# Two-layer hybrid decoder step: the first layer's projection opens with both slabs of its first pair, tile by tile

## The reference

```
mod = silu(c) @ ada_w[i] + ada_b[i]
h = rmsnorm(x, norm_pre_mix) * (1 + sc1) + sh1
proj = h @ w_in                       # gb, gc, hv, z (1024 each), xbc (1536), dt_raw (16)
xbc_c = silu(causal_conv4(xbc)); dt = softplus(dt_raw + dt_bias)
mix = concat(gb * causal_conv3(gc * hv), ssd(xbc_c, dt, ...)) @ w_out
x = x + g1 * rmsnorm(mix)
h = rmsnorm(x) * (1 + sc2) + sh2
f = swiglu(h) in layer 0, top-2-of-8 expert swiglu in layer 1
x = x + g2 * rmsnorm(f)
```

## Time and profile before

| What | Value |
|---|---|
| median of 3 executions | 2057.71 us (2055.87 to 2061.11) |
| profiled execution, its own time | 2059.96 us |
| span of the profiled execution | 2057.9 us |
| TensorE (matmul) busy | 1927.6 us, 94% |
| VectorE busy | 1233.8 us, 60% |
| ScalarE busy | 846.2 us, 41% |
| mean granted TensorE clock | 0.964 of full speed |

### The profile page before, as it was taken

One profiled execution on the slowest core, in us unless ns is written; L12 is line 12 of the kernel. 1 busy time (PEld: TensorE's weight loads), 2 busy tenths in 40 slices (PEclk: granted clock), 3 DMA queues, 4 the chain that ended last, 5 costly groups with the idle time before them and its releaser, 6 DMA issues.

```text
span 2057.9 us, 36163 instructions
## 1 busy us (share of the span) xinstructions
PE 1927.6 (94%) x13204; PEld 1716.4 (83%) x13204; DVE 1233.8 (60%) x1783; ACT 846.2 (41%) x1030; POOL 218.7 (11%) x317
## 2 busy tenths in 40 slices
PE   4999999999999999987999999996599999999994
PEld 3888998997999999986889989995487878888884
DVE  3677667645523232336776666656565566888886
ACT  4332222454422122234322222635355456777774
POOL 3101211200000000001102212100100000000020
PEclk8999999999999999997999999997699999999997
DMA  9642443354234333325624333423547567999994
GB/s 337 236 165 93 133 133 108 128 210 150 96 132 142 104 134 132 118 76 201 241 92 140 127 101 129 151 82 125 186 144 264 194 204 249 362 385 383 382 385 171
DMA packets 146670, 376.99 MB, mean 183 GB/s; under 512 B 9712, under 2 KB 47024, under 8 KB 146080
## 3 DMA queue, kind: packets, MB, share of 16 engines
q1 hardware_dynamic: 119824, 274.61, 38.8%
q0 software_dynamic: 26768, 101.28, 13.6%
HBM read 340.06 MB, written 35.80 MB: 183 GB/s over the span
## 4 chain that ended last, share of the span: by engine, by line
PE 85%; DVE 4%; issue 4%; DMA 3%; ACT 2%; POOL 1%; DVEq 0%; POOLq 0%; ACTq 0%; SPq 0%
PE ps L1913 35%; PE ps L1921 17%; PE ps L2235 17%; PE ps L2256 4%; PE ps L1956 2%; PE ps L2105 1%; DMA adaw<-w_ada 1%; PE ps L1966 1%; PE ps L1935 1%; PE ps L2108 1%; PE ps L2106 1%; PE ps L2093 1%; DMA rawr<-w_gu 1%; PE ps L1988 1%; POOL wreg L737 0%
## 5 line engine op out<-in xcount | busy, mean ns | idle before, releaser
L1913 PE MATMUL ps<-h_hi,whi 128*128 128x272 f32 x2304 | 485.2, 292 | 7.1 <-DVE h_lo L1236 7.1
L1913 PE MATMUL ps<-h_lo,whi 128*128 128x272 f32 x2304 | 479.1, 289 | 0.0
L1913 PEld LDWEIGHTS ps<-h_hi,whi 128*128 128x128 f32 x2304 | 363.5, 189 | 49.8 <-issue 29.5
L1746 DVE TENSOR_TENSOR wlr<-rawr,whr 128x2048 fp32r<-128x2048 f32 (+1 forms) x162 | 322.1, 1993 | 121.3 <-ACT whr L1041 117.7
L1184 DVE TENSOR_TENSOR wlo<-raw,whi 128x1024 fp32r<-128x1024 f32 (+1 forms) x180 | 229.3, 1274 | 255.2 <-ACT whi L781 252.7
L1913 PEld LDWEIGHTS ps<-h_lo,whi 128*128 128x128 f32 x2304 | 363.5, 189 | 0.0
L781 ACT CAST whi<-raw 128x1024 fp32r<-128x1024 f32 (+1 forms) x180 | 193.7, 1076 | 347.5 <-PE ps L1921 342.1
L1041 ACT CAST whr<-rawr 128x2048 fp32r<-128x2048 f32 (+1 forms) x162 | 269.1, 1667 | 155.6 <-PE ps L2256 87.6
L1921 PE MATMUL ps<-h_hi,wlo 128*128 128x272 f32 x2304 | 311.7, 288 | 0.0
L1921 PEld LDWEIGHTS ps<-h_hi,wlo 128*128 128x128 f32 x2304 | 297.9, 188 | 0.0
L2235 PE MATMUL ps<-whr,hu_hi 128*128 128x512 f32 (+1 forms) x432 | 168.3, 390 | 7.0 <-DVE yu L1810 4.5
(11 more groups left out here) (411 smaller groups left out, 2683.2 us busy)
## 6 DMA issues: line engine op xcount, KB each, us to landing
rawr<-w_gu SPq DMA_DIRECT2D x90, 1024.0 KB, 9.7
adaw<-w_ada POOLq DMA_DIRECT2D x48, 1024.0 KB, 8.9
rawr<-w_dn SPq DMA_DIRECT2D x54, 768.0 KB, 9.5
raw<-w_mix SPq DMA_DIRECT2D x64, 512.0 KB, 3.4
raw<-w_gu SPq DMA_DIRECT2D x44, 512.0 KB, 3.3
raw<-w_out SPq DMA_DIRECT2D x32, 512.0 KB, 3.3
y_rows<-tables POOLq DMA_DIRECT2D x26, 512.0 KB, 2.9
raw<-w_xbc SPq DMA_DIRECT2D x24, 512.0 KB, 3.8
```

Source lines behind the costliest of these rows:

```text
L1746: v.tensor_tensor(ring_group(wlr, g).rearrange("p k s c -> p s k c"), raw_group(g), ring_group(whr, g).bitcast(F32).rearrange("p k s c -> ...
L1913: mm(ps[:, 2 * s + half, 0:HALF], whi[:, s, k * P:(k + 1) * P], a[:, k, half * HALF:(half + 1) * HALF], start=(n < 2), stop=False)
```

## The change

```diff
@@ SyncE @@
                 if L == 0:
                     load_slab(0, 0, w_xbc[L, 0], SLAB)
-
-                    sp.wait_ge(ada_landed[KT - 2], 16)
                     load_slab(0, 1, w_xbc[L, 1], SLAB)
@@ ScalarE @@
                 make_rstd(NORMS * L + PRE_MIX, D, rstd)
                 if L == 0:
                     hi(0, 0, SLAB)
+                    hi(0, 1, SLAB)
                 modulate(L, 0, 0)
-                if L == 0:
-                    hi(0, 1, SLAB)
@@ VectorE @@
             lo(0, 0, SLAB)
+            lo(0, 1, SLAB)
...
                 dve.wait_ge(h_ready, (2 * L + 1) * KT)
-                if L == 0:
-                    lo(0, 1, SLAB)
                 narrow_take(L, 0)
@@ TensorE @@
-                        if L and i == 0:
+                        if i == 0:
                             if s == 0:
                                 first_pair(first["xbc"], h_ready, 2 * L * KT, lambda k: project(L, 0, k))
                                 by_token(L, 0, ps[:, 5, :]).then_inc(dt_done, 1)
-                        elif (i, s) == (0, 0):
-                            slab(first["xbc"], 0, KT, h_hi, h_lo, (h_ready, 2 * L * KT), lambda k: project(L, 0, k))
-                            by_token(L, 0, ps[:, 5, :]).then_inc(dt_done, 1)
                         else:
                             slab(i + first["xbc"], s, KT, h_hi, h_lo)
```

## The result

The changed kernel takes 2063.97 us (median of 20 executions, 2058.57 to 2070.49) against 2056.94 us of the kernel before (20 executions, 2052.0 to 2063.95): 7.0 us more by the medians. The ratio is 1.003, 95% interval 1.002 to 1.004, which is 4 to 8 us.

What follows compares the result with a forecast made beforehand. TensorE's chain was taken to bound the kernel, with the opening up to 35 us bound by full DMA engines. 1.36 + 0.4 + 2.3 + 3.0 = 7.06, taken as +7.1 on 2057.71, gave 2064.8 us, range 2060.0 to 2068.0.

Steps and rivals of the forecast that it cites:

- Part 1, bytes ahead of the last piece: Opening: slab (0, 1)'s 512 KB move ahead of the last `adaw` piece at 386 GB/s, delaying `mod` and first matmul, +1.36 us.
- Rival 3: Opening: GpSimd's queue sets the pace, so slab (0, 1) loads free and the piece still lands at 35.08; 2063.0 us, 5%.
- the sign that was named: Opening: the last piece of `adaw` lands at 36.4 to 37.2 us instead of 35.08.
- Part 1, the earlier slab (1, 0): Opening: slab (1, 0), issued earlier, shares the DMA engines with the last `adaw` piece, +0.4 us, upper end 2.7.
- Rival 2: Opening: SyncE's slabs take turns with the last piece from their issue on; landing beyond 38 us, 2067.1 us, 10%.
- Part 2, the splits: Ahead of `modulate`: ScalarE's second cast and VectorE's second subtraction fit in their idle time, 0 us.
- Part 3, the wait: Layer 0, TensorE's opening: only 2.84 us of work left over the 5.14 us dt chain, so +2.3 us waiting for `dA_ready`.
- Part 4, the clock: Layer 0 behind that wait: clock falls to 0.50, slowing the products of `dA` and slab (1, 0), +3.0 us.
- Rival 1: Behind layer 0's wait for `dA_ready`: the wait is too short for the clock to fall; 2061.8 us, 20%.
- What comes after: Behind slab (1, 0) and in later stages: the backlog makes no gap and the shift passes through, 0 us.
- the chances: Whole kernel, against a mark of 0.3% (6.2 us): slower 0.54, the same 0.44, faster 0.02.

## Why the prediction was right

The forecast was +7.1 us, 2064.8; measured were +7.0 and 2063.97. That the two agree to 0.1 us is luck: the interval is some 2 us wide on either side, the ratio alone gives 6.2 us, and a term that was too large stands beside a delay that was left out. The mechanism, bytes, wait and clock, held. Step by step:

- **Part 1, bytes ahead of the last piece: 1.36.** Right. The landing moved by 1.45 on the mean of four profiles against four, and by 2.74 for twice the bytes. Rival 3 (free beside GpSimd's queue) falls with that. With slab (1, 0) held back the step is 36.12 - 34.90 = 1.22. But the sign that was named, a landing at 36.4 to 37.2 us, was missed: it came at 36.09, and in the three runs that also load early at 36.31, 36.34 and 36.64. The sign had the 0.4 of the next item in it, and it started from 35.08, the latest of the four landings without the early load.
- **Part 1, the earlier slab (1, 0): 0.4, bounds 0 to 2.7.** Too large. Holding it back moved the landing by 0.2 us on the mean, within the scatter. Its bytes came about as late as supposed: issued from 31.58 us on, none before 35 us, 0.14 MB before 36 us. Rival 2 (turns from the issue on, beyond 38 us) falls. By the rule of the Trainium skill (DMA: Bandwidth & Descriptors, Queues, rings and completion order) the queues take turns; here the trace agrees for 16 to 20 us (52.2% and 50.2%) and 36 to 42 us (56.2% and 45.2%), and not for the first 3 to 4 us behind the issue.
- **Not in the sum: the clock before the first tile.** With the piece later, the eight matmuls on it mostly ran wholly at half clock (1.98 us), and the first matmul on `h` moved by 1.8 us on the mean where the landing moved by 1.4. The 0.4 us more have the size of the charge for slab (1, 0), by another cause, and scatter as much as it.
- **Part 2, the splits: 0.** Right for the time: ScalarE's and VectorE's idle time ahead of `modulate` covered them; both were done by 32.6 us.

```profile
29.11 1.98 ACT L779 CAST whi<-raw 128x1024 fp32r<-128x1024 f32 x2
30.17 2.36 DVE L1181 TENSOR_TENSOR wlo<-raw,whi 128x1024 fp32r<-128x1024 f32 x2 [13.08 <-ACT whi L779]
```

- **Part 3, the wait: 2.3.** Right: 68.52 - 63.37 = 5.15, less 2.84 of `ada_w`, is 2.31. With the order alone it comes, without any change to the loads. The view of waits lists 2.5, because the three pieces, run one behind the other, took 2.7 instead of 2.84. Whether taking both slabs tile by tile gains something in itself stays open to 0.4 us. From the first matmul on `h` to the end of the main pass the four profiles that do it took 14.06 us on the mean, which leaves 9.84 without the 4.22 of slab (0, 1); the six others took 10.28, and either group spreads over 0.8 us.
- **Part 4, the clock: 3.0.** Right for layer 0: (72.47 - 68.52) - 2.26 = 1.69 in the products and (80.05 - 72.47) - 6.23 = 1.35 in slab (1, 0), 3.04 together; filling the wait gave 2.95 back. Rival 1 (the wait is too short for a fall) did not occur: the clock fell behind each of the nine waits of this kind in the profiles of before, after and the runs here. But the price is not fixed. In eight of them the stretch took 16.5 to 16.7 us, in one, layer 1 of the changed kernel, 15.21 (987.14 - 971.93), where the fall came only as slab (1, 0) began and lasted half as long, for a reason that no run here shows:

```profile
977.30:979.90 2.60, 2.60 (x18) 1.83 (x18) 2.02 (x6) 0.96 (x2) 0.00 (x0) 1.00 1.03 400
980.00:983.40 3.40, 3.40 (x17) 3.40 (x16) 2.97 (x5) 1.25 (x3) 0.00 (x0) 0.50 0.92 346
983.50:985.00 1.50, 1.50 (x14) 1.50 (x14) 1.16 (x5) 0.76 (x1) 0.00 (x0) 1.00 0.46 115
```

- **What comes after: 0.** Right: the slab behind the pieces starts at 81.90 without a gap, and the medians carry the whole sum.

With the measured sizes the sum is 1.45 + 2.31 + 3.04 = 6.8 us, against 7.0 measured with some 2 us of interval on either side. The halves timed apart, +1.6 and +5.0 by medians, add up to 6.6. In the one pair of profiles the steps up to the end of slab (1, 0) add up to less: +0.23 at the first matmul on `h`, -0.69 from there to the end of `by_token` (19.16 - 6.21 against 13.64), +5.33 behind it, 4.87 us. The first two are as small as that because of the clock in these two executions: it stayed up over the last piece here and not there, and was back at 1.00 by 48.2 us here and by 49.1 there.

One sum of the prediction is wrong: its bounds within the forecast, 1.7 to 3.5 for the clock and 0 to 0.7 for slab (1, 0), give 5.4 to 7.9 us with the other terms, and not 8.3. The measured 7.0 lies in both, and the chances hardly change.

## What to carry to other kernels

Before a block of work is moved on the busiest engine, ask what chain on the other engines it was lying over; here 9.05 us of matmuls had covered a chain of 5.1 us, and the 6.2 us of them that moved ahead of the chain's start covered nothing. The producer of a side chain's input goes as early as its data allow: here between two passes of matmuls, worth 4.7 us in a layer that had the fault already. A stage that ends on a transfer at full bandwidth pays for each byte that is put ahead of it, whichever queue carries it. If the same order of work already runs elsewhere in the program, its rows price the change better than a sum of parts.

## What was not expected

- Matmuls without any use, put into a wait of 2.5 us, made the changed kernel about 6 us faster: waits of 2.5 us cost more by the clock behind them (3.0 us each in eight of nine) than by the time that they add (2.3 us).
- The early load of one slab, 1.45 us later on the chain, can't be told in 12 timed executions (interval -0.06% to +0.17%), while the landing in the row of the chain for `adaw` separates the five profiles with it (36.09 us or more) from the four with the old loads (35.08 or less).
- Two profiles of kernels that differ by 7 us in the median had spans within 0.2 us of each other; TensorE's busy time for the same matmuls was 6.0 us less in the slower kernel's.
